# Neighbourhood limits kept in the bias tables, and scores that keep their sign

## The reference

```
s_loc = einsum(q, k_window) * d ** -0.5
s_loc = s_loc + bias                        # learned, by row and column offset
s_loc = where(in_win, s_loc, -1e30)         # 16 columns around the query
s_ctx = einsum(q, k_ctx) * d ** -0.5
p     = softmax(concat([s_loc, s_ctx]))
o     = p_loc @ v_window + p_ctx @ v_ctx
```

## Time and profile before

| | us |
|---|---|
| median of 3 runs | 2006.2 (2004.68 to 2007.41) |
| the profiled execution | 2007.27 |
| its span | 2005.4 |
| first scores of the attention stage | 226.72 |
| scores of step 4, the first latent one | 242.22 |
| scores of step 19, the last | 397.53 |
| fetch of the first expert's rows issued; the expert stage follows | 472.71 |

### The profile page before, as it was taken

One profiled execution on the slowest core, in us unless ns is written; L12 is line 12 of the kernel. 1 busy time (PEld: TensorE's weight loads), 2 busy tenths in 40 slices (PEclk: granted clock), 3 DMA queues, 4 the chain that ended last, 5 costly groups with the idle time before them and its releaser, 6 DMA issues.

```text
span 2005.4 us, 25015 instructions
## 1 busy us (share of the span) xinstructions
PE 1937.0 (97%) x9564; PEld 1325.9 (66%) x9564; DVE 1646.9 (82%) x1625; ACT 1379.2 (69%) x1618; POOL 191.6 (10%) x100
## 2 busy tenths in 40 slices
PE   8999889985999999999999999999999999999998
PEld 7999666653666666666666666666666666666664
DVE  3766556677988989898989898988989898989896
ACT  3222256645787777878787878787787878787875
POOL 0000212123010101010100101010101010110100
PEclk9999799996999999999999999999999999999999
DMA  9534601145999999999999999999999999999993
GB/s 379 202 153 174 219 27 58 54 137 172 386 352 404 372 390 376 382 379 373 390 362 395 351 403 353 402 358 384 373 386 379 368 390 366 393 358 399 353 389 153
DMA packets 100997, 636.32 MB, mean 317 GB/s; under 512 B 11568, under 2 KB 19760, under 8 KB 28048
## 3 DMA queue, kind: packets, MB, share of 16 engines
q1 hardware_dynamic: 96048, 618.23, 78.9%
q0 software_dynamic: 4832, 16.50, 3.1%
HBM read 620.02 MB, written 13.88 MB: 316 GB/s over the span
## 4 chain that ended last, share of the span: by engine, by line
PE 75%; ACT 1%; DVE 0%; issue 0%; DVEq 0%; ACTq 0%
PE ps L1447 16%; PE ps L1446 16%; PE ps L1451 16%; PE ps L1463 8%; PE ps L1464 8%; PE ps L1468 8%; PE ps L1426 1%; PE ps L1417 0%; DVE place L1611 0%; ACT place L1543 0%; PE ps L1486 0%; ACT place L1546 0%; ACT L1546 0%; ACT place L1498 0%; ACT place L1541 0%; DVE place L1608 0%
## 5 line engine op out<-in xcount | busy, mean ns | idle before, releaser
L675 DVE TENSOR_TENSOR place<-ring,place 128x2048 fp32r<-128x2048 f32 x526 | 1222.3, 2336 | 146.3 <-ACT place L671 142.1
L671 ACT ACTIVATE place<-ring 128x2048 fp32r<-128x2048 f32 x528 | 1010.0, 1916 | 312.2 <-PE ps L1451 235.4
L1446 PE MATMUL ps<-place 128*80 128x512 f32 x1408 | 561.1, 399 | 1.8 <-DVE place L1554 1.8
L1447 PE MATMUL ps<-place 128*80 128x512 f32 x1408 | 555.6, 395 | 0.0
L1451 PE MATMUL ps<-place 128*80 128x512 f32 x1408 | 381.4, 392 | 0.0
L1451 PEld LDWEIGHTS ps<-place 128*80 128x80 f32 x1408 | 208.3, 148 | 115.7 <-issue 0.7
L1463 PE MATMUL ps<-place 128*80 128x512 f32 x704 | 280.5, 398 | 0.0
L1447 PEld LDWEIGHTS ps<-place 128*80 128x80 f32 x1408 | 209.4, 149 | 107.0 <-issue 0.7
L1446 PEld LDWEIGHTS ps<-place 128*80 128x80 f32 x1408 | 208.5, 148 | 107.3 <-DVE place L1554 2.0
L1464 PE MATMUL ps<-place 128*80 128x512 f32 x704 | 277.2, 394 | 0.0
L1468 PE MATMUL ps<-place 128*80 128x512 f32 x704 | 190.4, 392 | 0.0
(11 more groups left out here) (190 smaller groups left out, 1714.6 us busy)
## 6 DMA issues: line engine op xcount, KB each, us to landing
ring<-in_w_exp SPq DMA_DIRECT2D x528, 1024.0 KB, 7.0
ring<-in_w_late SPq DMA_DIRECT2D x16, 1024.0 KB, 9.9
ring<-in_w_in SPq DMA_DIRECT2D x12, 1024.0 KB, 6.9
ring<-in_w_ada SPq DMA_DIRECT2D x8, 1024.0 KB, 10.7
ring<-in_w_out SPq DMA_DIRECT2D x4, 1024.0 KB, 6.3
place<-in_near_bias SPq DMA_DIRECT2D x16, 256.0 KB, 3.1
ring<-in_xT SPq DMA_DIRECT2D x4, 640.0 KB, 9.9
place<-in_x SPq DMA_DIRECT2D x5, 512.0 KB, 6.4
```

The lines of the kernel that those rows point to most:

```text
L671: eng.activation(wH[:, n % SPLITS, :], ring[:, slot("exp", n), :], ACT.Copy).then_inc(wh_done, 1)
L675: eng.tensor_tensor(wL[:, n % SPLITS, :], ring[:, slot("exp", n), :], wH[:, n % SPLITS, :].bitcast(F32), ALU.subtract).then_inc(chunk_used, 1)
L1446: eng.matmul(out, xH[:, e % 2, kk, :], w, start=(kk == 0), stop=False)
L1447: eng.matmul(out, xL[:, e % 2, kk, :], w, start=False, stop=False)
```

## The change

The bias table comes from the host with the limits in it: inside the window it is the bias, outside it is -1e30. `far`, its load, and GpSimd's `finish_tab` are gone. The queries keep their sign, VectorE adds the table and takes the maximum, and since the exponential wants the negated maximum, one more instruction negates the two (128x2). For that each of the two additions is chained. The additions wait for the load itself (`tab_landed`) and for the zeros (`tab_zero`), where they waited for GpSimd (`tab_done`). The negation counts for both in `max_done`.

```
-                    dst, sc = ((qna, -SCALE), (kna, 1.0), (qdf, SCALE), (kdf, 1.0))[g]
+                    dst, sc = ((qna, SCALE), (kna, 1.0), (qdf, SCALE), (kdf, 1.0))[g]
...
-        far = take(3 * NEAR).rearrange("p (c n) -> p c n", c=3)
...
-                eng.dma_start(far, a["far"].rearrange("c p n -> p c n")).then_inc(far_landed, 16)
...
-                def finish_tab(u):
-
-                    t, i = unit(u)
-                    eng.wait_ge(tab_landed[u % 3], 16 * ((u - GROUPS) // 3 + 1))
-                    tab = tabs[:, u % 3, :, 0:NEAR]
-                    eng.tensor_tensor(tab, far[:, KINDS[t - 1]:KINDS[t - 1] + 1, :].broadcast_to([P, 2, NEAR]), tab,
-                                      ALU.subtract).then_inc(tab_done, 1)
-
                 eng.memset(tabs[:, :, :, NEAR:], 0.0).then_inc(tab_zero, 1)
-                eng.wait_ge(far_landed, 16)
-                finish_tab(GROUPS)
-                finish_tab(GROUPS + 1)
...
                 for k in range(STEPS):
-                    if GROUPS + 2 <= k + 1 < UNITS:
-                        finish_tab(k + 1)
...
                     eng.activation(probs(u, part, t), columns(part, t), ACT.Exp, bias=stat[:, u, part:part + 1],
-                                   scale=-1.0 if part < 2 else 1.0, accum_out=total[:, u, part:part + 1]
+                                   accum_out=total[:, u, part:part + 1]
                                    ).then_inc(p_done, 1)
...
                         if t:
-                            eng.wait_ge(tab_done, u - GROUPS + 1)
-                            eng.tensor_tensor_reduce(src, src, tabs[:, u % 3, m, :], 1.0, 3e38, ALU.add, ALU.min,
-                                                     out).then_inc(max_done, 1)
+                            eng.wait_ge(tab_zero, 1)
+                            eng.wait_ge(tab_landed[u % 3], 16 * ((u - GROUPS) // 3 + 1))
+                            chain(eng.tensor_tensor_reduce(src, src, tabs[:, u % 3, m, :], 1.0, -3e38, ALU.add, ALU.max, out))
                         else:
-                            eng.tensor_reduce(out, src, AX_X, ALU.min).then_inc(max_done, 1)
+                            eng.tensor_reduce(out, src, AX_X, ALU.max, negate=True).then_inc(max_done, 1)
                     if t:
+                        eng.tensor_scalar(stat[:, u, 0:2], stat[:, u, 0:2], -1.0, None, ALU.mult).then_inc(max_done, 2)
                         eng.wait_ge(s_ready, waits + 1)
```

More of the change, by code:

```diff
@@ L561, in build @@
         v_shifted = sem("v_shifted")
-        far_landed = sem("far_landed")
         tab_landed = [sem(f"tab_landed{i}") for i in range(3)]
         tab_zero = sem("tab_zero")
-        tab_done = sem("tab_done")
         ln_landed = sem("ln_landed")
@@ L1624, in near_bias @@
     row = s[None, :] - r[:, None] + WIN_H - 1
+    w = np.arange(GRID)
+    c0 = np.clip(w - WIN_W // 2, 0, GRID - WIN_W)
+    inside = (w[None, :] >= c0[:, None]) & (w[None, :] < c0[:, None] + WIN_W)
     tabs = []
-    for shift in SHIFTS:
+    for kind, shift in enumerate(SHIFTS):
+        b = KINDS.index(kind)
+        near = inside[b * TILE_COLS:(b + 1) * TILE_COLS, KEY_COL0[b]:KEY_COL0[b] + KEY_COLS]
+        near = np.repeat(np.repeat(near, ROWS, axis=0), ROWS, axis=1)
         col = np.clip(shift + j[None, :] - i[:, None], 1 - WIN_W, WIN_W - 1) + WIN_W - 1
-        tabs.append(rpb[:, row, col].transpose(1, 0, 2))
+        tabs.append(np.where(near[:, None, :], rpb[:, row, col].transpose(1, 0, 2), np.float32(-FAR)))
     return np.stack(tabs, axis=0)
@@ L1648, in constants @@
     sin = np.concatenate([np.sin(ang).T, np.sin(ang).T], axis=0)
[L1649 to L1657, removed]
     return {
@@ L1663, in constants @@
         "sinT": np.ascontiguousarray(sin, dtype=np.float32),
-        "far": np.stack(far, axis=0),
     }
```

## The result

The changed kernel took 2015.77 us (median of 5 runs, 2014.19 to 2017.9), the kernel before 2007.06 us in the same job (2004.68 to 2009.05). The ratio is 1.0044, its 95% interval 1.0033 to 1.0055: 0.44% slower, 8.7 us, where 0.07% was forecast. The time lies outside the range, and a slowing by over 0.2% had been given a chance of 0.07.

A forecast was written before the change was run, and what follows sets the result against it. TensorE was taken to bound the kernel. The terms, 1.26 and 0.06 us, made it 1.3 us longer, from a median of 2006.2 to 2007.5 us; range 2004.0 to 2011.0 us.

The forecast's parts named there:

- GpSimd's tables: Sixteen table instructions, 20 us of GpSimd in all, go; nobody waits for them, so the gain is zero.
- L1160 of steps 9 and 13: VectorE instruction slowed beside GpSimd's tables; would fall to 0.69 us, a gain counted as zero on the path.
- rival 1: What stands behind L1160 reaches TensorE, giving back 1.5 us in steps 9 and 13: 2006.0 us; chance 0.08.
- the wait for L1157 in steps 9, 13 and 17: TensorE already waits there for VectorE to empty the projection's bank, so 3 x 0.42 = 1.26 us lands on the path.
- Steps 11 and 15: TensorE comes late to the projection there, a cover of 0.46 us, so the 0.42 us does not show.
- Step 6: No projection runs beside it; of 0.42 us some 0.36 is covered, leaving 0.06 us.
- The 0.08 us for a signal: Taken off the 0.44 us between the maximum's end and ScalarE's table load in step 6.
- The length of the maxima: VectorE's maxima in latent steps become 0.35 to 0.48 us longer, taken as 0.42; bounds 0.15 and 0.60.
- the price of the negation: The added 128x2 instruction in VectorE's maxima, put at 0.15 us from a subtraction on 128x16.
- the lock: A VectorE instruction with two SBUF inputs waits for a GpSimd instruction that reads SBUF, for its whole duration.
- Rival 2: ScalarE's lateness reaches TensorE in all 16 latent steps, 6.7 us: 2012.9 us; chance 0.05.
- the ordinary steps: Steps 7, 8, 10, 12, 14, 16, 18: the projection's matmuls give 1.7 us of cover, so the cost is zero.

The follow-up runs named there:

- chain_only: The kernel before, with a wait for its own completion behind each of the two bias additions; 2008.82 us, ratio to before 1.0006.
- neg_reduce: The changed kernel, with the negation written as a reduction over one element in place of the multiplication by -1; 2009.32 us, ratio to before 1.0009.
- filled: The changed kernel, with eight unread products put on TensorE before the projection's half in steps 13 and 17; 2015.91 us, ratio to before 1.0044.
- spare_neg: The kernel before, with an unread 128x2 multiplication by -1 in SBUF added in each latent step, without a wait; 2015.47 us, ratio to before 1.0046.
- after_sum: The changed kernel, with GpSimd's layer norm instructions of the third tile held until VectorE has scaled the last heads; 2015.94 us, ratio to before 1.0038.
- between_gate_sum: Kernel of between, with L1157 ahead of the maxima in steps 9, 13, 17 and GpSimd's third-tile layer norm held; 2004.20 us, ratio to before 0.9983.
- before_gate: The kernel before, with VectorE emptying the projection's bank ahead of the maxima in steps 9, 13 and 17; 2003.53 us, ratio to before 0.9981.
- between: The changed kernel, with unchained additions and the negation as a reduction between the two wide maxima; 2014.67 us, ratio to before 1.0038.
- between_sum: The kernel of between, with GpSimd's layer norm of the third tile held until the last heads are scaled; 2009.36 us, ratio to before 1.0002.
- sum_late: The changed kernel, with GpSimd's layer norm of the first two tiles held until the bank is emptied in steps 13 and 17; 2008.81 us, ratio 1.0009.

## Why the prediction was wrong

*What held.* GpSimd's tables were on nobody's path: with the bank emptied first, the intervals overlap whether GpSimd makes them or not. L1160 of steps 9 and 13 takes 0.69 us, as said, and TensorE gained nothing by it (rival 1 falls). The path is the wait for L1157 in steps 9, 13 and 17, and there the loss sits. Step 9 is the forecast's own case: TensorE idles 1.21 us, where 1.2 to 1.3 was said, and the step is 0.46 us longer. Steps 11 and 15, with 0.46 us of cover, show 0.06. Step 6, counted at 0.06, shows 0.01 (11.37 for 11.36). The 0.08 us for a signal in that term is in no run, and the reading there was off: ScalarE was busy with a copy until 263.02, so its table load at 263.04 did not wait for the maximum.

*The length of the maxima.* Put at 0.35 to 0.48 us; without a collision it is 0.46 (in step 8 of the changed kernel from 281.56 to 283.02, 1.46 for 1.00). The two chained waits are 0.31 of it by run chain_only, where I had 0.20 to 0.24, and the negation the rest. The Trainium skill's rule (VectorE: DVE Perf Modes, section "The DRAIN you can't avoid"), that a semaphore between two Vector instructions costs nothing extra, does not hold for these: about 0.15 us for each wait behind an accumulator read.

*The step that failed* is the price of the negation: "The negation works on 128x2; the nearest row, a subtraction on 128x16, starts 0.15 us before its successor". That subtraction reads PSUM. The negation reads and writes SBUF, and this decides, since there it competes with GpSimd. The trace of before had the row that would have told it, GpSimd in step 13:

```profile
332.87 2.36 POOL L758 TENSOR_TENSOR place<-place 128x1024 f32<-128x1024 f32 x1
```

It spans just the time at which the negation was to stand, 333.5 to 333.9. In before only instructions with a PSUM source stood there (bias additions, maxima), and those pass GpSimd: the second addition takes 0.60 us there and 0.56 to 0.60 anywhere, the two maxima 1.55. I named the lock and the page that states it (SBUF — State Buffer, section "Who interferes with whom"), but looked only at what the change frees from it, not at the instruction that the change puts into it. The same section says that a multiplication by a constant can take the port that GpSimd shares and that a reduction never does. The trace agrees with both: 1.33 and 1.43 us against 0.15. From the first addition to the wide maxima it was 2.64 us in step 13 and 2.73 in step 17, where the sum had 1.42 in all three steps.

*The term that was missing* is TensorE's clock. I priced each microsecond of idle time at a microsecond. In steps 13 and 17 another 1.56 and 1.68 us went because the work behind ran at 0.50 of the clock; the sum had nothing for it.

By the lengths of the steps the loss in the profiled execution divides like this. The maxima: 0.46 in step 9, 0.36 and 0.37 in steps 13 and 17 (run neg_reduce, 12.87 and 12.88, less 12.51), in all 1.2 us, where 1.26 was said. The collision: 14.06 and 14.16 (run filled) less 12.87 and 12.88, 1.2 and 1.3, in all 2.5 us. The clock: 15.62 and 15.84 less 14.06 and 14.16, in all 3.2 us. Together 6.9, of 6.8 measured. This rests on one execution of each kernel, and elsewhere differences of up to 0.4 us happen to cancel.

Rival 2 named the right order of loss (2012.9) for the wrong reason: nothing was lost in the ordinary steps.

*What stays open.* The medians differ by 8.7 us and the profiled spans by 6.8. Within one job the lowest and the highest run of one kernel lie 3.7 us apart (the changed kernel, 5 runs) to 11.4 (before, 33 runs). Much of what differs between traces lies in steps 5 and 6, where the clock is low in before too: together they took 19.5 us in spare_neg, 21.1 in the changed kernel and 23.3 in after_sum, which differs from it only behind step 19. I have not shown that this makes up the rest. Step 7 varies as well, and not with the tables: 9.6 us in before and in between_gate_sum, 10.4 in before_gate, 11.0 in between. Its low clock begins in step 6, behind waits of TensorE of 1.55 and 0.89 us that before has too. Why the clock fell in step 9 of between and between_sum, where TensorE idled 0.81 us for 0.75 in before, was not found.

## What to carry to other kernels

Before adding a small VectorE instruction, ask where its operands lie and what GpSimd runs at that time: with SBUF on both sides, 0.17 us became 1.4, and the same numbers as a reduction took 0.15. Look for the one place where TensorE already waits; there nearly all of a lengthening is paid (0.36 to 0.46 of 0.46 us), and idle time there (2.4 us here) can be paid again in clock, so the cure that paid best here was to put the instruction that TensorE waits for ahead of those it doesn't. And taking work from an engine that nobody waits for was worth nothing here; what the work was replaced by was the whole price.

## What was not expected of the hardware

- The clock did not follow the length of TensorE's idle time alone. It fell after 2.43 us (step 13 of the changed kernel), stayed after 2.41 (step 17 of spare_neg) and after 1.27 (sum_late). And it fell after 0.81 (step 9 of between and again of between_sum) where 0.89 in before left it.
- The wait works in both directions: in run sum_late, where GpSimd's two products start amid VectorE's gated half and the difference of the two maps, they take 2.83 and 2.81 us and not 2.35.
- A collision of an instruction with three parts (three scalings in a row, 0.88 us) cost 4.3 us, as it met two GpSimd instructions one behind the other (422.06 to 426.89 in between).
